# Expert tokens by one-hot products from rows kept in SBUF, residual through DRAM, in a hybrid decoder layer with 32 experts

## What is computed

```
h = rmsnorm(x1) * (1 + sc2) + sh2                  # 264 x 1024
logits = h @ w_router + b_router                   # top 4 of 32, softmax over the 4
gu = xb @ w_gate_up[e] + b_gate_up[e]              # xb: the rows of h of expert e
act = clamp(gl) * sigmoid(1.702 * gl) * (clamp(up) + 1)
y_e = act @ w_down[e] + b_down[e]
x = x1 + gt2 * rmsnorm(sum of gate * y_e, g_post_ffn)
```

## Time and profile before

| | |
|---|---|
| median of 3 runs | 1600.42 us |
| the profiled execution's own time | 1601.76 us |
| its span, first to last instruction | 1599.9 us |
| TensorE busy | 1417.5 us (89%), 6825 matmul records |
| VectorE, ScalarE, GpSimd busy | 582.9, 274.4, 71.2 us |
| moved by DMA | 510.72 MB, of it 498.06 MB on SyncE's queue, 8.91 MB on GpSimd's |
| mean granted TensorE clock | 0.949 of 2.4 GHz |
| chain that ended last | TensorE 56%, DMA 35%, VectorE 4%, issue 3% |

### The profile page before, as it was taken

How to read it: one execution, slowest core, us unless ns; L and a number is a source line. 1 busy time by engine, 2 the same in 40 slices (tenths; PEclk the granted TensorE clock), 3 DMA queues, 4 the chain that set the end, 5 groups by cost and what they waited for, 6 DMA issues and landing times.

```text
span 1599.9 us, 17465 instructions
## 1 busy us (share of the span) xinstructions
PE 1417.5 (89%) x6825; PEld 771.5 (48%) x6825; DVE 582.9 (36%) x1518; ACT 274.4 (17%) x575; POOL 71.2 (4%) x53
## 2 busy tenths in 40 slices
PE   5999999999799958999989888888699988888886
PEld 2878899877566743343333333233233323323323
DVE  2455987779432162334323112112121211211214
ACT  2324311121241121111111111110011111101111
POOL 1000000234000000000000000000000000000000
PEclk8899998999899968899999999999799999999999
DMA  9432440221675817999999999999999999999993
GB/s 391 193 144 105 158 145 1 82 78 53 268 304 204 351 63 308 403 428 428 426 426 429 426 427 427 427 410 411 426 428 426 428 427 427 427 428 427 427 428 150
DMA packets 40799, 510.72 MB, mean 319 GB/s; under 512 B 5864, under 2 KB 6504, under 8 KB 10512
## 3 DMA queue, kind: packets, MB, share of 16 engines
q1 hardware_dynamic: 36480, 498.06, 74.8%
q0 software_dynamic: 2464, 8.91, 1.5%
q10 hardware_dynamic: 1776, 2.65, 0.5%
HBM read 501.16 MB, written 8.45 MB: 319 GB/s over the span
## 4 chain that ended last, share of the span: by engine, by line
PE 56%; DMA 35%; DVE 4%; issue 3%; ACT 1%; POOL 0%; SPq 0%; ACTq 0%; DVEq 0%; POOLq 0%
DMA ring<-experts_dram 20%; PE ps L806 13%; PE ps L498 9%; PE ps L814 8%; PE ps L546 8%; DMA spare<-experts_dram 7%; DMA work<-experts_dram 6%; PE ps L792 2%; PE ps L685 2%; PE ps L671 1%; PE ps L505 1%; PE ps L688 1%; PE ps L562 1%; PE ps L820 1%; DMA ring<-mix_dram 1%
## 5 line engine op out<-in xcount | busy, mean ns | idle before, releaser
L806 PE MATMUL ps<-ring,XT 128*64 128x512 f32 x1056 | 247.7, 613 | 46.0 <-DMA ring<-experts_dram 45.4
L1686 DVE TENSOR_TENSOR hT<-ps,btab 128x256 f32<-128x256 f32 x64 | 27.2, 425 | 489.2 <-PE ps L820 489.1
L806 PEld LDWEIGHTS ps<-ring,XT 128*64 128x64 f32 x1056 | 74.7, 140 | 205.4 <-issue 142.0
L498 PE MATMUL ps<-hT,ring 128*128 128x264 f32 x640 | 150.0, 395 | 0.0
L806 PE MATMUL ps<-spare,XT 128*64 128x512 f32 x544 | 126.0, 604 | 20.5 <-DMA spare<-experts_dram 20.5
L806 PE MATMUL ps<-work,XT 128*64 128x512 f32 x512 | 119.3, 608 | 27.1 <-DMA work<-experts_dram 16.2
L498 PEld LDWEIGHTS ps<-hT,ring 128*128 128x128 f32 x640 | 124.6, 195 | 22.5 <-issue 0.5
L1621 DVE TENSOR_TENSOR yacc<-yacc,ps 128x264 f32<-128x264 f32 x128 | 54.9, 429 | 177.1 <-PE ps L792 176.0
L814 PE MATMUL ps<-ring,AT 128*64 128x512 f32 x512 | 116.9, 598 | 1.6 <-DMA ring<-experts_dram 1.6
L1295 DVE SCALAR_TENSOR_TENSOR cvT<-uP,pv,cvT 128x256 f32<-128x256 f32 x240 | 99.7, 484 | 0.0
L546 PE MATMUL ps<-hT,ring 128*128 128x264 f32 x384 | 89.8, 389 | 0.0
(11 more groups left out here) (364 smaller groups left out, 1495.3 us busy)
## 6 DMA issues: line engine op xcount, KB each, us to landing
ring<-experts_dram SPq DMA_DIRECT2D x98, 2048.0 KB, 34.8
spare<-experts_dram SPq DMA_DIRECT2D x50, 2048.0 KB, 34.7
work<-experts_dram SPq DMA_DIRECT2D x50, 2048.0 KB, 35.2
ring<-mix_dram SPq DMA_DIRECT2D x32, 2048.0 KB, 8.5
ring<-sdn_dram SPq DMA_DIRECT2D x2, 2048.0 KB, 7.3
s_sample_dram<-ring SPq DMA_DIRECT2D x2, 2048.0 KB, 6.8
hT<-xT_dram SPq DMA_DIRECT2D x1, 1056.0 KB, 9.7
qT<-xT_dram SPq DMA_DIRECT2D x1, 1056.0 KB, 11.2
```

The lines of the kernel that those rows point to most:

```text
L498: mm = pe.matmul(ps[:, n % 2, 0:NT], ring[:, PLACE[j], k, (n % CPB) * P:(n % CPB + 1) * P], hT[:, k, :], start=(k == 0), stop=(k == KD - 1))
L806: mm = pe.matmul(ps[CAP * h:CAP * (h + 1), j, :], x, w[:, h * UW + (k % 4) * 512:h * UW + (k % 4 + 1) * 512], start=(k == 0), stop=(k == K ...
L1686: dve.tensor_tensor(glu, both[:, :, 0, :], bias(0), ALU.add).then_inc(chain, 1)
```

## The change

`rows_of` holds the token-major rows in SBUF: 256 rows take the place of x1 in `qT`, the 8 sample rows go to a new tile `srow`. `rows_in` no longer transposes gathered rows; it multiplies the kept rows with the one-hot matrix of the pair, for every 128 x 128 piece three products (tokens 0 to 127, 128 to 255, 256 to 263) that add up in PSUM. The store of `h2rows`, all indirect gathers, `slot_row`, and the four overflow tables go away. The one-hot matrices of four experts must now live until their pairs have been fetched, so `one_hot(g)` and table g stand later (`LATER`, `SIDE`). x1 is stored to a DRAM scratch `x1` as soon as it is complete, ScalarE waits for that store before it overwrites `qT`, and x1 is loaded back behind the last weights into the slot that is free then.

```diff
@@ -269,7 +265,9 @@
-        rowbuf = [yw[:, 0, :], yw[:, 1, :], G[:, :, :].rearrange("p a n -> p (a n)")]
+        x1_rows = qT[:, :, :].rearrange("p k n -> p (k n)")[:, 0:2 * D].rearrange("p (t n) -> p t n", t=2)
+        rows_of = [x1_rows[:, 0, :], x1_rows[:, 1, :], srow[0:NDE, :]]
+        ohot = hot[:, 1, :, 0, :]
...
-        for at, kinds in ((-1, (("table", 0),)),
-                          (0, (("table", 1), ("gates", 0))), (1, (("table", 2),)),
-                          (2, [("table", 3)] + [("bias", m) for m in range(4)]),
-                          (3, [("table", 4)] + [("bias", m) for m in range(4, KD)])):
+        for at, kinds in ((-1, (("table", 0),)), (0, (("gates", 0),)), (1, ()),
+                          (2, [("bias", m) for m in range(4)]), (3, [("bias", m) for m in range(4, KD)])):
...
-        for at, g in ((4, 5), (5, 6), (6, 7), (16, 8), (17, 9), (18, 10), (19, 11)):
-            SIDE[at] = [("table", g)]
+        for g in range(1, E // GRP):
+            SIDE[2 * GRP * g - 4].append(("table", g))
...
+        x1_place = position(E - 1, PARTS - 1) + 1
+        x1 = slot[x1_place % SLOTS][:, 0:KD * NT].rearrange("p (k n) -> p k n", k=KD)
@@ -454,8 +452,9 @@
-            sp.wait_ge(rows_out[1], 16)
-            sp.dma_start(bdn, A["bdn"]).then_inc(in_moe, 16)
+            sp.wait_ge(x1_ready, KD)
+            sp.dma_start(A["x1"], qT[:, :, :].rearrange("p k n -> p (k n)")).then_inc(x1_out, 16)
+            sp.dma_start(bdn, A["bdn"]).then_inc(in_bdn, 16)
...
+            sp.wait_ge(part_used, x1_place - SLOTS + 1 - PARTS)
+            sp.wait_ge(x1_out, 16)
+            sp.dma_start(slot[x1_place % SLOTS][:, 0:KD * NT], A["x1"]).then_inc(x1_in, 16)
@@ -794,12 +796,15 @@
-                pe.wait_ge(xg_in, 16 * (p + 1))
+                pe.wait_ge(hot_ready, 2 * p // GRP + 1)
...
                 for k in range(4):
-                    tr = pe.transpose(ps[:, 7, k * P:(k + 1) * P], Xg[:, (4 * q + k) * P:(4 * q + k + 1) * P], ident)
-                tr.then_inc(xt_done, 1)
+                    for t, (t0, m) in enumerate(TILES):
+                        mm = pe.matmul(ps[:, 7, k * P:(k + 1) * P], rows_of[t][:, (4 * q + k) * P:(4 * q + k + 1) * P],
+                                       hot[0:m, p // 2 % 2, t, 2 * (p % 2):2 * (p % 2) + 2, :].rearrange("p e n -> p (e n)").bitcast(F32),
+                                       start=(t == 0), stop=(t == 2))
+                mm.then_inc(xt_done, 1)
@@ -855,11 +860,16 @@
-                pe.wait_ge(o_xg, 16 * b + 16)
+                pe.wait_ge(o_hot, b + 1)
                 for k in range(KD):
-                    tr = pe.matmul(ps[:, 7, CAP * k:CAP * (k + 1)], Xg[0:CAP, k * P:(k + 1) * P], ident[0:CAP, 0:CAP],
-                                   start=True, stop=True)
-                tr.then_inc(o_xt, 1)
+                    for t, (t0, m) in enumerate(TILES):
+                        mm = pe.matmul(ps[:, 7, CAP * k:CAP * (k + 1)], rows_of[t][:, k * P:(k + 1) * P], ohot[0:m, t, :].bitcast(F32),
+                                       start=(t == 0), stop=(t == 2))
+                mm.then_inc(o_xt, 1)
+                for t, (t0, m) in enumerate(TILES):
+                    mm = pe.matmul(ps[0:CAP, 5, 0:3], ohot[0:m, t, :].bitcast(F32), otg[0:m, t, :].bitcast(F32),
+                                   start=(t == 0), stop=(t == 2))
+                mm.then_inc(o_tab, 1)
@@ -1127,12 +1137,11 @@
+            act.wait_ge(x1_out, 16)
             for t, (t0, m) in enumerate(TILES):
                 act.wait_ge(tm_done, t + 1)
                 b0 = 4 + 2 * (t % 2)
-                act.activation(rowbuf[t][0:m, :], ps[0:m, b0:b0 + 2, :].rearrange("p b n -> p (b n)"), ACT.Copy).then_inc(tm_copied, 1)
-                act.wait_ge(tm_copied, t + 1)
-                act.dma_start(A["h2rows"][t0:t0 + m, :], rowbuf[t][0:m, :]).then_inc(rows_out[t], 16)
+                act.activation(rows_of[t], ps[0:m, b0:b0 + 2, :].rearrange("p b n -> p (b n)"), ACT.Copy).then_inc(tm_copied, 1)
@@ -1670,10 +1671,10 @@
 -            LATER = {0: [lambda: one_hot(3), lambda: one_hot(4)], 1: [lambda: one_hot(5), lambda: one_hot(6)],
-                     2: [lambda: one_hot(7), overflow_blocks], 3: [overflow_owner], 4: [lambda: overflow_rows(0)],
...
+            LATER = {2: [overflow_blocks], 3: [overflow_owner], 4: [lambda: overflow_rows(0)], 6: [lambda: overflow_rows(1)],
+                     7: [lambda: overflow_rows(2)], 8: [lambda: gates(slice(E, NBLK), gov[:, :, :])]}
+            for g in range(1, E // GRP):
+                LATER[GRP * g - 3] = [lambda g=g: one_hot(g)]
...
-            dve.tensor_tensor(yacc[:, :, NPR:NT], yacc[:, :, NPR:NT], qT[:, :, NPR:NT], ALU.add)
+            dve.wait_ge(x1_in, 16)
+            dve.tensor_tensor(yacc[:, :, NPR:NT], yacc[:, :, NPR:NT], x1[:, :, NPR:NT], ALU.add)
@@ -1790,45 +1797,7 @@
-            for p in range(MID // 2 + 1):
-                gather(p)
-                pool.wait_ge(xg_in, 16 * (p + 1))
...
-                gather_extra()
...
-            for p in range(MID // 2 + 1, PAIRS):
-                gather(p)
-                pool.wait_ge(xg_in, 16 * (p + 1))
```

More of the change, by code:

```diff
@@ L1180, in extra @@
                 rows_back(1, 0).then_inc(o_y, 1)
-            for t in range(3):
-                act.wait_ge(rows_out[t], 16)
             rows_up(0, 0)
@@ L1602, in take @@
                             tab = out[CAP * r:CAP * (r + 1), 0:3 * GRP].rearrange("p (g a) -> p g a", a=6)
-                            if x < E // GRP:
-                                dst = [a[CAP * r:CAP * (r + 1), GRP // 2 * x:GRP // 2 * (x + 1)]
-                                       for a in (slot_tok, slot_row, slot_gate)]
-                            else:
-                                c0 = GRP * x - E
-                                dst = [a[:, c0:c0 + GRP].rearrange("p (g b) -> p g b", b=2)[:, :, r]
-                                       for a in (o_tok, o_row, o_gate)]
-                            dve.tensor_copy(dst[1], tab[:, :, 3 * r])
+                            dst = [a[CAP * r:CAP * (r + 1), GRP // 2 * x:GRP // 2 * (x + 1)] for a in (slot_tok, slot_gate)]
                             dve.tensor_copy(dst[0], tab[:, :, 3 * r])
-                            lk(dve.tensor_copy(dst[2], tab[:, :, 3 * r + 1]))
-                            ins = dve.tensor_tensor(dst[2], dst[2], tab[:, :, 3 * r + 2], ALU.add)
+                            lk(dve.tensor_copy(dst[1], tab[:, :, 3 * r + 1]))
+                            ins = dve.tensor_tensor(dst[1], dst[1], tab[:, :, 3 * r + 2], ALU.add)
                     elif kind == "gates":
@@ L1713, in extra @@
                 dve.tensor_copy(bcol[:, :], btab[:, bass.ds(e * (2 * KD), 2 * KD)])
-                dve.tensor_copy(ocol[:, 0:1], o_tok[:, bass.ds(b, 1)])
-                dve.tensor_copy(ocol[:, 1:2], o_gate[:, bass.ds(b, 1)]).then_inc(o_chain, 1)
+                dve.tensor_copy(orank[:, :], rk[:, :, bass.ds(b + E, 1)].rearrange("p t o -> p (t o)"))
+                dve.tensor_copy(otg[:, :, :], tg[:, :, bass.ds(b + E, 1), :].rearrange("p t o a -> p t (o a)")).then_inc(o_chain, 1)
                 dve.wait_ge(o_chain, (LINKS + 1) * b + 1)
+                dve.wait_ge(xt_done, 2 * (MID // 2))
+                for t in range(3):
+                    ins = dve.tensor_scalar(ohot[:, t, :], cxc("iota")[:, 0:CAP], orank[:, t:t + 1], None, ALU.is_equal)
+                ins.then_inc(o_hot, 1)
+                dve.wait_ge(o_tab, b + 1)
+                dve.tensor_copy(ocol[:, :], ps[0:CAP, 5, 0:2]).then_inc(o_col, 1)
+                dve.wait_ge(o_col, 2 * b + 1)
+                dve.tensor_tensor(ocol[:, 1:2], ocol[:, 1:2], ps[0:CAP, 5, 2:3], ALU.add).then_inc(o_col, 1)
+                dve.wait_ge(o_col, 2 * b + 2)
                 placing(place[0:CAP, 1, :], ocol[:, 0:1], ocol[:, 1:2]).then_inc(o_place, 1)
@@ L1726, in _ @@
             take(-1)
-            dve.wait_ge(side_taken, 1)
-            dve.memset(s3[0:1, 1, 0:1], 0.0).then_inc(tab_ready, 1)
-            one_hot(1)
-            one_hot(2)
             bias_plus_one()
@@ L1792, in _ @@
             pool.wait_ge(h2_ready, 1)
-            pool.memset(o_row[:, OVF:OVF + 1], 0)
             pool.memset(r3[:, 0, :, :], 0.0).then_inc(memset_done, 1)
-            def gather(p):
-                pool.wait_ge(tab_ready, 1)
-                if p >= 1:
-                    pool.wait_ge(xt_done, 2 * p)
-                    pool.wait_ge(side_taken, NTH["table", p * 2 // GRP] + 1)
-                pool.indirect_dma_start(out=Xg[:, :], out_offset=None, in_=A["h2rows"],
-                                        in_offset=bass.IndirectOffsetOnAxis(ap=slot_row[:, p:p + 1], axis=0)).then_inc(xg_in, 16)
-            def gather_extra():
-                pool.indirect_dma_start(out=Xg[0:CAP, :], out_offset=None, in_=A["h2rows"],
-                                        in_offset=bass.IndirectOffsetOnAxis(ap=idxc[:, :], axis=0)).then_inc(o_xg, 16)
-            def extra(b):
```

(23 more changed lines are left out.)

30 lines of the change are left out of this document (12 added, 18 removed).

## The result

The changed kernel takes 1608.53 us (median of 9 executions, 1603.88 to 1609.65) against 1601.74 us for the kernel before on the same chips: a ratio of 1.0038 (1.0028 to 1.0048), slower by 0.4% where 1571 us and faster was forecast. Its profiled execution took 1609.53 us, with a span of 1607.7. Eight megabytes have left the DMA queues (510.72 MB became 502.96) and GpSimd's queue is empty, so the change did what it says; the time went elsewhere.

A forecast was written before the change was run, and what follows sets the result against it. Weight transfers were taken to bound the expert stage. Savings of 21.8 (pair gathers) + 4.6 (overflow gathers) + 3.3 (start) + 0 (TensorE) = 29.7 us, from 1600.4, gave 1571 us, range 1564 to 1588.

The forecast's parts named there:

- TensorE's added work: In each expert pair: 48 records at 0.111 us replace 8 transposes, +4.4 us, hidden behind the weight transfers, cost 0.
- the gathers: In the transfer stream: dropping 14 pair gathers at 1.56 us saves 21.8 us, two overflow gathers at 2.3 save 4.6.
- The slack: Per pair in the expert stage: TensorE needs 53.8 us, twelve weight parts take 58.8, so 5.0 us remain.
- The rival "TensorE becomes the bound": In the 48 records per pair: TensorE's own path sets the end and the kernel gets slower; chance 0.07.
- The turn: In the pairs: the kernel becomes slower once 8.7 us are added a pair, 0.20 us a record.
- The start: From table 0 to the first slot request: 3.3 us gained, between -1.2 and +5.3.
- come back 4 us in: At the start: full clock returns 4 us into the products of `rows_in`, leaving half the first batch slow.
- The overflow block: Between the pairs: its 54 records take 6 us instead of 2.0, absorbed with 6.7 us margin, cost 0.
- x1: Storing x1 and loading it back, 2 x 1.08 MB: costs nothing, covered by gaps of 11 us and more.

The follow-up runs named there:

- the padded products: Changed kernel with the third product per piece, and the overflow block's, on 128 rows instead of 8, the rest zeroed: 1575.94 us, ratio 0.9842.
- the run: Kernel before with its first gather alone, all pairs working on the first pair's rows: 1580.33 us, ratio 0.9868.
- the run above: Changed kernel with ten extra products of ones and identity behind the rank products: median 1611.05 us, ratio 1.0038.

## Why the prediction was wrong, step by step

- **TensorE's added work** is the step that failed: "48 records at 0.111 = 5.3 us, against 8 transposes, 0.9: +4.4 ... hidden". The pitch came from sixteen records of one shape; of the 48, sixteen have 8 rows. With 0.20 us a change they take 8.04 us, +7.1 a pair. With them on 128 rows the step is right, and the kernel takes 1575.9 us, within the range. That is 32.6 of the 37.5 us between the forecast and the measured time; the other 4.9 are less than the 7 by which the gathers were read too high (below).
- **The slack.** I compared a pair's 53.8 us with its 58.8 of stream. TensorE's own path, which I worked out for the rival only, was 1469 us, but its 16 x 49.4 = 790 left out the tables and bias products inside the loop. Measured: start 614.1 + pairs 917.4 (490.7 + 426.7) + overflow 55.2 + tail 21.0 = 1607.7 us. The pairs' 127 us above 790 are 15 x 7.1 = 107 of the change and, by difference, 20 of that side work (seven tables at 58.3 - 56.7 = 1.6 us are 11 of them). The turn lay at (131 - 20) / 15 = 7.4 us a pair, not 8.7, and with 9.3 us lost at the start (0.6 a pair) it was passed. The rival "TensorE becomes the bound" had place and mechanism, and a chance of 0.07 because its price was tested with the shape that has no change in it.
- **The start.** Forecast a gain of 3.3, between -1.2 and +5.3; measured a loss of 6.1 behind table 0. Even the lower bound had the clock's doubling only (12.2 us for both halves); at the low clock with the changes they took 16.3 (597.84 to 614.10). That the clock would "come back 4 us in" held for the padded products, which began at 595.92 and had it back in 599 to 600, and not for these.
- **The overflow block.** "Cost 0" assumed 6.7 us of margin, with the stream busy through the block. With TensorE leading, a longer block counts in full: 2.3 us, at the low clock for part of it (with its products on 128 rows it takes 5.5 less than before). The stream lost 16.6 us of transfer beside it.
- **The gathers.** 26.4 us forecast for 14 pair gathers and the two of the overflow; 20.7 measured for these and the second pair's. Bytes at 428 GB/s give 19.6. By 0.406 MB a us those of the forecast cost 19.4, so 1.56 and 2.3 a gather were together read 7 us too high; the run does not part the two.
- **x1** out and back cost nothing, as said: nobody waits for it in the trace.

## What to carry to other kernels

A pitch holds for the shape and the neighbours it was read from: with a remainder tile, price the changes between its operands' height and the others', or pad it with zeros to 128 rows, which cost nothing here. And when a transfer-bound kernel gets work for another engine, sum that engine's whole path, side work and start included, against the end; the slack of one period does not tell.

## What the runs showed of the hardware

- A change between operands of 128 rows and of 8 rows costs 0.20 us at full clock (3.45 us with 4 changes in a half, 4.02 with 8 of which 7 lie inside it, 2.68 with none), and 32 or 64 rows give the same half of 4.02 and 4.03 us; the height itself costs nothing. The Trainium skill, TensorE: Matmul & The Clock Gate, section Why this matters for your kernels, has a single product on 32 rows take the time of one on 128; the records here agree, as long as no change stands between.
- One-hot products that alternate heights stayed at the low clock for 15 us (0.50 in 600 to 615, with two pauses of under 1 us), and fell to it from full clock in the run above; with the same count on 128 rows the clock rose at 599 to 600. In the overflow block, too, every version with 8 rows there fell to 0.50 within the 48 one-hot records (changed kernel: 0.52 in 1110 to 1115), which took 9.3 to 10.3 us, and every version with 128 rows there ran them in 5.6 at 1.00. Yet the same alternation in the later pairs ran at 1.00 (1060 to 1080): it can go with a falling clock and need not. The router's products (128 rows, 32 moving columns) stayed at 0.50 through their 8 us in every run, and the clock rose in the transposes behind them: in the kernel before these begin at 585.87 and it rose in 589 to 590, in the changed kernel at 587.78 and 591 to 592.
- Gathers of 4 KB rows on the GpSimd queue beside a full stream cost 20.7 us for 8.40 MB, some 5% more than their bytes at the stream's 428 GB/s.
